# Differential attention by pairs of heads with tokens on the partitions, and a merge that projects its gates ahead of its values

## The reference, cut to what matters

```python
def diffattn_prep(q, k, v, q_norm_w, k_norm_w, rope):
    qh = rmsnorm(q.reshape(bsz, n, B_HEADS, 2, B_QK), q_norm_w)      # B_QK = 64: two maps per head
    kh = rmsnorm(k.reshape(bsz, n, B_HEADS, 2, B_QK), k_norm_w)
    if rope is not None:                                             # latent tokens alone
        qh, kh = apply_axial_rope(qh, rope), apply_axial_rope(kh, rope)
def attend(q, k, v, lam):
    s = einsum('bhmqd,bhmkd->bhmqk', q, k) * (B_QK ** -0.5)
    p = softmax(s, axis=-1)
    w = p[:, :, 0] - lam * p[:, :, 1]
    return einsum('bhqk,bhkv->bhqv', w, v)                           # 128 values per head
def diffattn_out(o, subln_w, lam_init):
    return rmsnorm(o, subln_w) * (1.0 - lam_init)
y_b = diffattn_out(o_b, subln_w, lam_init) * silu(bz)
y = sigmoid(g_a) * (y_a @ w_a_out) + sigmoid(g_b) * (y_b @ w_b_out) + sigmoid(g_c) * (y_c @ w_c_out)
```

## Time and profile before

| | us |
|---|---|
| median of three runs | 2843.8 |
| the profiled execution's own time | 2846.33 |
| its span | 2844.5 |
| branch B and its merge, layer 0, from the first q to the first projection of branch C | 465.7 to 947.6 |
| the same, layer 1 | 1509.5 to 1814.7 |

### The profile page before, as it was taken

How to read it: one execution, slowest core, us unless ns; L and a number is a source line. 1 busy time by engine, 2 the same in 40 slices (tenths; PEclk the granted TensorE clock), 3 DMA queues, 4 the chain that set the end, 5 groups by cost and what they waited for, 6 DMA issues and landing times.

```text
span 2844.5 us, 38559 instructions
## 1 busy us (share of the span) xinstructions
PE 2526.8 (89%) x16000; PEld 2196.4 (77%) x16000; DVE 1299.1 (46%) x2636; ACT 1061.0 (37%) x1815; POOL 850.0 (30%) x554
## 2 busy tenths in 40 slices
PE   6999899988869999968989987997888999888998
PEld 3877778766647888758878776997867899857998
DVE  4322222555542111453234665226665675565673
ACT  3233322433431232333334444443344444354443
POOL 2222222221112233223233222443312354312453
PEclk9899899999979999979989998998999999989999
DMA  6211134111103312222223211444313354402444
GB/s 235 78 60 60 45 119 158 65 45 45 45 30 124 143 60 89 82 78 90 75 91 132 75 66 54 149 143 156 129 49 119 119 179 171 147 36 91 162 171 141
DMA packets 50414, 291.79 MB, mean 103 GB/s; under 512 B 8960, under 2 KB 13184, under 8 KB 19072
## 3 DMA queue, kind: packets, MB, share of 16 engines
q1 hardware_dynamic: 50240, 289.33, 28.6%
HBM read 287.21 MB, written 2.36 MB: 102 GB/s over the span
## 4 chain that ended last, share of the span: by engine, by line
PE 73%; DVE 13%; ACT 7%; issue 2%; POOL 2%; DMA 2%; SPq 1%; DVEq 0%; ACTq 0%; POOLq 0%
PE PS L430 72%; ACT wh L1207 3%; ACT TM L1197 2%; DVE TM L1693 2%; DMA raw<-in_wpk 2%; DVE wl L1712 1%; PE PS L434 1%; POOL wl L2392 1%; DVE TM L1701 1%; POOL TM L2384 1%; DVE small L1697 1%; DVE colS L1701 1%; DVE colS L1974 1%; ACT wh L1208 1%; DVE HYl L1701 1%
## 5 line engine op out<-in xcount | busy, mean ns | idle before, releaser
L430 PE MATMUL PS<-HYh,wh 128*128 128x256 f32 (+1 forms) x3512 | 1155.9, 329 | 65.2 <-DVE HYl L1701 23.1
L430 PE MATMUL PS<-HYl,wh 128*128 128x256 f32 (+1 forms) x3512 | 1132.9, 323 | 0.0
L430 PE MATMUL PS<-HYh,wl 128*128 128x256 f32 (+1 forms) x3512 | 1132.0, 322 | 0.0
L2392 POOL TENSOR_TENSOR wl<-raw,wh 128x768 fp32r<-128x768 f32 (+2 forms) x254 | 578.1, 2276 | 1502.2 <-ACT wh L1208 1502.1
L430 PEld LDWEIGHTS PS<-HYh,wh 128*128 128x128 f32 x3512 | 684.0, 195 | 147.8 <-issue 34.2
L1712 DVE TENSOR_TENSOR wl<-raw,wh 128x1280 fp32r<-128x1280 f32 (+2 forms) x254 | 368.9, 1452 | 767.4 <-ACT wh L1207 767.4
L430 PEld LDWEIGHTS PS<-HYh,wl 128*128 128x128 f32 x3512 | 683.0, 194 | 46.5
L430 PEld LDWEIGHTS PS<-HYl,wh 128*128 128x128 f32 x3512 | 684.5, 195 | 43.1
L1207 ACT ACTIVATE wh<-raw 128x1280 fp32r<-128x1280 f32 (+2 forms) x254 | 306.1, 1205 | 371.6 <-PE PS L430 208.4
L1197 ACT ACTIVATE TM<-PS 128x512 f32<-128x512 f32 (+4 forms) x323 | 164.6, 520 | 738.5 <-PE PS L430 614.5
L430 PE MATMUL PS<-TM 128*128 128x256 f32 (+4 forms) x688 | 220.8, 528 | 95.9 <-DVE TM L1701 53.8
(11 more groups left out here) (155 smaller groups left out, 2205.2 us busy)
## 6 DMA issues: line engine op xcount, KB each, us to landing
raw<-in_wpk SPq DMA_DIRECT2D x235, 1024.0 KB, 4.8
raw<-in_wpk SPq DMA_DIRECT2D x32, 704.0 KB, 4.1
TM<-in_wpk SPq DMA_DIRECT2D x4, 1024.0 KB, 18.7
X<-in_xin SPq DMA_DIRECT2D x1, 2048.0 KB, 10.3
Y<-in_wpk SPq DMA_DIRECT2D x2, 1024.0 KB, 23.7
Y<-bias_d SPq DMA_DIRECT2D x4, 512.0 KB, 10.0
raw<-in_wpk SPq DMA_DIRECT2D x3, 512.0 KB, 3.8
T<-in_tabs SPq DMA_DIRECT2D x1, 1216.0 KB, 15.3
```

The costliest lines, as they stand in the source:

```text
L430: return P.x.matmul(o, l, r, start=start, stop=stop)
L2392: G.x.tensor_tensor(wl[:, s, c:n], raw[:, r, c:n], wh[:, s, c:n], ALU.subtract).then_inc(*lo_rest.mark(u))
```

## The change

Branch B now goes by pairs of heads (p = 0 to 3), with units `b_q`, `b_k`, `b_v`, `b_z` of 256 features each, all projected by `proj_k` in chunks of 128 tokens: 16 chunks per pair in layer 0, 12 in layer 1 (q and z of the latent tokens alone). The norms are then sums along the free axis on VectorE (no `sums`, no `spread`), the rotary embedding is products on GpSimd with tables laid out per token (the features of a head are reordered in the weights so that its halves are contiguous), q and k are transposed by TensorE, v isn't. The values have the weights' transposes as the stationary operand, so that the output has queries on the partitions; its norm is a per-partition scale, and the result is transposed for the merge. Silu and Sigmoid are made from Tanh (the factor of one quarter is in `b_scale`).

The slot tables say which tile is issued in which slot: in layer 0 a tile's scores every second slot, its transposes two slots later, its values three; in layer 1 every third slot, with the same two and three. For the last pair (from its second tile) they lie in the merge, a tile per slot in layer 0 and every second slot in layer 1. The merge `merge_b` projects its eight gates first, a slot before each, and then the values; the first two values leave out the last head's part until it is there.

The table of constants is no longer 768 columns from memory: the small columns are set by memset, and the first load brings 128 columns. A new buffer `wtab` of 512 columns holds the rotary tables per token.

```diff
+        for p in range(4):
+            for tag, base in (("b_q", 4112), ("b_k", 5136)):
+                add(tag, [("w_in", l, [base + 256 * p + 64 * i + d for i in range(4) for d in halves])])
+            for tag, base in (("b_v", 6160), ("b_z", 7184)):
+                add(tag, [("w_in", l, r(base + 256 * p, base + 256 * p + 256))])
+        for j in range(4):
+            add("m_b", [("w_in", l, r(11280 + 256 * j, 11536 + 256 * j))])
...
+        for j in range(4):
+            add("m_b", [("w_b_out", l, r(256 * j, 256 * j + 256))])
...
+        B_PER, B_LAG, B_NT = (16, 12), (14, 11), (4, 2)
...
+            kinds = [("q", t) for t in range(i0, 4)] + [(x, t) for x in "kv" for t in range(4)] + [("z", t) for t in range(i0, 4)]
...
+        def b_score_slot(l, p, j):
+            n = B_PER[l] * p + B_LAG[l] + (2, 3)[l] * j
+            if p == 3 and j:
+                n = 63 + j if l == 0 else 47 + 2 * j
+            return n
+        def b_turn_slot(l, p, j):
+            return b_score_slot(l, p, j) + (1 if l == 0 and p == 3 and j else 2)
+        def b_value_slot(l, p, j):
+            return b_turn_slot(l, p, j) + 1
...
+        B_QK = ({12: 0, 14: 1}, {10: 0, 11: 1})
```

TensorE, a pair's slots and chunks:

```diff
+                for n in range(B_BASE[l]):
+                    p, kind, t_ = b_chunk(l, n)
+                    i, half = divmod(t_, 2)
+                    slot_b(l, n)
+                    if (a := B_QK[l].get(n % B_PER[l])) is not None:
+                        for c, x in enumerate("qk"):
+                            P.wait_ge(pool_step, ("b_ready", l, p, x, 1))
...
+                                t = turned(bank(6 + c)[:, 128 * tt:128 * tt + 128], b_qn[c][:, tt, 128 * a:128 * a + 128])
...
+                    u = place["b_" + kind, 4 * l + p]
+                    proj_k(bank(b)[:, 256 * half:256 * half + 256], u, H, h_ready(l), 8, 128 * t_, ("b_" + kind, l, p, t_),
+                           *([("unit", u)] if t_ == 3 else []))
```

VectorE, `slot_b(l, n, chunk)` with `chunk` = n - 1, in this order on the engine (after `b_exp` come the reciprocal, the product with lambda, the tensor_scalar and the scalar_tensor_tensor as before, which give `b_w`):

```diff
+                if pj := B_SCORES[l].get(n):
+                    D.x.reduce_max(st[:, 32:34], PS[:, 2:4, 0:nk], AX).then_inc(*dve_step.mark())
+                    D.wait_own(dve_step)
+                    ts(st[:, 34:36], st[:, 32:34], -0.125, None, ALU.mult, None, ("b_nb", l, *pj))
+                if chunk is not None:
+                    chunk_b(l, chunk)
+                if pj := B_TURNS[l].get(n + 1):
+                    D.wait_ge(act_step, ("b_exp", l, *pj))
...
+                if (pj := B_VALUES[l].get(n)) and pj[1] % B_NT[l] == B_NT[l] - 1:
+                    D.wait_ge(act_step, ("b_osq", l, *pj))
+                    root(small[:, 40:40 + nt], small[:, 44:44 + nt], colC[:, 32:32 + nt])
...
+                    for i in range(nt):
+                        stt(b_yt[:, i], bank(5)[:, 128 * i:128 * i + 128], small[:, 40 + i:41 + i], b_z[p % 2][:, 2 * l + i, a], ALU.mult, ALU.mult,
+                            ("b_yo", l, p, a))
+            def chunk_b(l, n):
+                if t_ % 2:
+                    if kind in "qk":
+                        D.wait_ge(act_step, ("b_sq", l, p, kind, i))
+                        D.x.reduce_sum(ss[:, 8 * i:8 * i + 8], qn[i], AX).then_inc(*dve_step.mark())
+                        if i:
+                            root(colS[:, z0:16], colS[:, 16 + z0:32], ss[:, z0:16])
+                            for x in range(z0 // 8, 2):
+                                tt(qn[x], wide(bank(b_bank(l, kind, x))), colS[:, 8 * x:8 * x + 8].unsqueeze(2).to_broadcast([128, 8, 64]),
+                                   ALU.mult, ("b_norm", l, p, kind, x))
+                    elif kind == "z":
+                        stt(zt, zt, 1.0, src, ALU.add, ALU.mult, ("b_z", l, p, i))
+                if t_ == 3:
+                    used("b_" + kind, 4 * l + p)
```

GpSimd, after the last chunk of a q or a k: one product of 512 columns (context half), four of 128 (the exchanged halves), two of 256, one sum of 512 (`b_ready`), and then the conversion of its share of a unit:

```diff
+                            tt(x, x, ones(b_w[:, c], 8), ALU.mult)
...
+                                tt(m2[:, :, s_], x[:, :, 1 - s_], b_tab[:, c, 1, t, 32 * s_:32 * s_ + 32].unsqueeze(1).to_broadcast([128, 4, 32]), ALU.mult)
...
+                            tt(x, x, ones(b_tab[:, c, 0, t], 4), ALU.mult)
...
+                        tt(b_qn[c][:, 2:4], b_qn[c][:, 2:4], b_m2, ALU.add, ("b_ready", l, p, kind, 1))
+                    if t_ == 3:
+                        used("b_" + kind, 4 * l + p)
```

ScalarE squares q and k (Square, 512 columns), copies v, makes z's Tanh, each followed at a kind's last chunk by its conversion (`used`); then in the slot it copies the transposed output, the transposed weights, makes the exponentials, and squares a tile's output with its sum (`b_osq`), in this order. The merge on TensorE:

```diff
+                for j in range(8):
+                    u = place["m_b", 8 * l + j // 2]
+                    slot_b(l, base + j)
...
+                    proj_t(bank(j % 2)[:, 0:N], u, 128 * (j % 2), 128, H, h_ready(l), 0, 8, t0, N, ("m_gate", l, "b", j),
...
+                for j in range(2):
+                    slot_b(l, base + 8 + j)
+                    value(u, j, range(7))
+                slot_b(l, base + 10)
+                for j in range(2):
+                    value(u, j, range(7, 8))
...
+                for j in range(2, 8):
+                    value(u, j, range(8))
...
-            S.x.dma_start(T[:, 0:768], tabs[:, 0:768]).then_inc(*consts_in.mark("first", by=16))
+            S.x.dma_start(ident, tabs[:, 0:128]).then_inc(*consts_in.mark("first", by=16))
```

More of the change, by code:

```diff
@@ L52, in merge @@
                 ada(q)
+    halves = [32 * g + 16 * s + k for s in range(2) for g in range(2) for k in range(16)]
     for l in range(2):
@@ L67, in plan_units @@
         merge("a", 10256)
[L68 to L73, removed]
+        for p in range(4):
[5 more added lines that the diff above has]
+            add("m_b", [("w_in", l, r(11280 + 256 * j, 11536 + 256 * j))])
+            if l == 0:
+                ada(ada_at(l, "b", j))
+        for j in range(4):
+            add("m_b", [("w_b_out", l, r(256 * j, 256 * j + 256))])
+            if l == 0:
+                ada(ada_at(l, "b", 4 + j))
         for g in range(4):
@@ L251, in tab @@
             return T[:, at[0] - n:at[0]]
-        ident, o1024, o64, o128, o256, one = (tab(128) for _ in range(6))
+        ident, o1024, o64, o128, o256, one = (tab(n) for n in (128, 1, 2, 1, 4, 4))
         CS = tab(1536).rearrange("p (t c) -> p t c", t=2)
@@ L387, in b_kept @@
[L387 to L391, removed]
+        b_qn = [tm(1024 * c, [4, 256]) for c in range(2)]
+        b_m2 = tm(2048, [2, 256])
+        b_qt = [tm(2560 + 1024 * a, [2, 512]) for a in range(2)]
+        b_v = [tm(4608 + 1024 * i, [4, 2, 128]) for i in range(2)]
+        b_z = [tm(6656 + 1024 * i, [4, 2, 128]) for i in range(2)]
+        b_wt = [tm(8704 + 512 * i, [512]) for i in range(2)]
@@ L1184, in tensor_program @@
                 branch_b(l)
[L1185 removed]
+                merge_b(l)
                 branch_c(l)
@@ new lines, in branch_b @@
+            def branch_b(l):
+                li = 0.8 - 0.6 * math.exp(-0.3 * l)
+                ts(small[:, 34 + l:35 + l], vcol(f"sub{l}"), 0.25 * (1.0 - li), None, ALU.mult, None, ("b_scale", l))
+                D.wait_ge(pe_step, ("b_tables", l))
+                if l == 0:
+                    cp(b_cs.rearrange("p s t d -> p (s t d)"), bank(6)[:, 0:256])
+                else:
+                    D.wait_ge(pool_step, ("b_ready", 0, 3, "k", 1))
+                cp(perm1, bank(6)[:, 256:384], ("b_tables", l))
+                for n in range(B_BASE[l]):
+                    slot_b(l, n, n - 1 if n else None)
@@ L2349, in second_block @@
                 low(name, 7)
+            D.x.memset(o64, 0.0).then_inc(*dve_step.mark())
+            D.wait_own(dve_step)
+            for i in range(2):
+                D.x.memset(o64[64 * i:64 * i + 64, i:i + 1], 1 / 64).then_inc(*dve_step.mark("halves"))
             D.wait_ge(consts_in, "first")
@@ L2582, in pool_program @@
                 branch_b(l)
-                merge(l, "b")
+                merge_b(l)
                 branch_c(l)
```

632 lines of the change are left out of this document (336 added, 296 removed).

## The result

The changed kernel takes 2796.7 us (median of 4 runs, 2790.7 to 2797.7) against 2843.6 (4 runs, 2841.7 to 2844.8): a ratio of 0.9831, 95% interval 0.9814 to 0.9848. It is faster by 47 us, 1.7%, where I forecast 115, and it lies outside my range of 2672 to 2770. The profiled execution took 2796.6 us, its span is 2794.8.

What follows compares the result with a forecast made beforehand. TensorE, busy 89% of the span, was taken as the bound, with its waits and the slow clock after them. Savings of 101 us (layer 0), 13 (layer 1) and 0.5 (table load) gave 115: median 2729 us, range 2672 to 2770.

Steps and rivals of the forecast that it cites:

- Part 2: Branch B's merges: the drain goes, as tiles fit between gates; 6 us of waits left in each merge.
- stretch like 812 to 857: Layer 0's drain before the change: 45.5 us, 19.5 busy, clock 0.64; slots 34 to 40 without projection; forecast to vanish.
- rival (e): Drain stays because the merge's order fails; layer 1 keeps 10 and layer 0 26 us of idling; 2775 us, chance 0.07.
- Part 1: TensorE's work in branch B at full pace: layer 0 from 396 to 362 us, layer 1 from 263 to 235.
- Part 3: Layer 0's pairs: waits behind VectorE's q and k work, 3.3 us per pair, 10 in three; layer 0 takes 381.
- Part 4: Layer 1's pairs: VectorE's queue causes waits of 8, 3.4 and 1.8 us per pair; layer 1 takes 292 us.
- the one I named: Layer 1's pairs: TensorE waits 7 to 8 us before a weights' transpose for VectorE's scalar_tensor_tensor, three times.
- rival (a): Layer 1's waits don't bite because VectorE's chain is shorter than summed; 2680 us, chance 0.17.
- rival (c): Tanh is not in Exp's table set, so slots reload tables, some 25 us; 2754 us, chance 0.05.
- Part 5: GpSimd's rotary products take 5.8 us per q or k, upper bound some 12; ScalarE is not near.
- rival (d): GpSimd becomes the bound through its q and k products, slower than before; about 2860 us, chance 0.03.
- Rival (b): VectorE is later than summed through more waits for GpSimd, 50 us, half on TensorE's path; 2755 us, chance 0.13.

Runs made afterwards that it cites:

- e3: Changed kernel with ScalarE's and VectorE's conversions of the merge's next unit moved behind the following slot; 2746.1 us, ratio 0.9652.
- e2: Changed kernel with VectorE's joining of the two maps ahead of its work on z, q and k in a slot; 2766.0 us, ratio 0.972.
- e8: Changed kernel with the drain put back: all the last pair's slots issued before the merge's first gate; 2788.5 us, ratio 0.9806.
- e9: Changed kernel with only VectorE's conversion in the merge moved behind its slot, ScalarE's left in place; 2783.6 us, ratio 0.9785.
- e1: Changed kernel with layer 0's merge doing the `ada` units before gates 0, 2, 4, 6 instead of after 1, 3, 5, 7; 2757.2 us, ratio 0.9696.
- e6: Changed kernel with the edits of e3 and e2 together, but the merge's first slot in the old order; 2710.4 us, ratio 0.9533.
- e7: As e6, with VectorE's conversion of `b_q` and `b_k` one slot later, behind the next joining; 2707.0 us, ratio 0.9519.

## Why the prediction was wrong

**The step that failed is Part 2's "I leave 6 us of waits in each merge".** The drain did go, and no stretch like 812 to 857 is left, but TensorE waits 29.4 us in layer 0's merge and 14.6 in layer 1's (2.5 of them just before its gate 0), and runs slow behind them. I had listed for each tile its chain of scores, maximum, exponentials and joining (5.7 us of 8.1), and I had put one conversion of VectorE into the account. I did not put in ScalarE's conversion, nor ask when the load that it waits for lands. In the kernel before, these conversions waited for their loads too. Between 812 and 947.6 us there are seven such waits; six of them, of 7.5 to 7.8 us, stand between gates and values, with no slot behind them. The first lies in the drain, and TensorE waits behind it (ScalarE's conversion, and TensorE's next instruction):

```profile
820.29 1.27 ACT L1207 ACTIVATE wh<-raw 128x1280 fp32r<-128x1280 f32 x1 [8.05 <-DMA raw<-in_wpk]
```

```profile
823.10 1.87 PE L430 MATMUL PS<-T,TM 128*128 128x1 f32 x8 [10.32 <-ACT TM L1197]
```

So some 8 of the 26 us of idle time that I put down to slots without a projection between them were a late load already, and the trace of before had shown the cost that I left out. Moving work behind a waiting instruction made its wait critical. My own rival (e), 2775, with chance 0.07, is nearest in kind, and I had no mechanism for it: its price of 26 us of idling for layer 0 was about right (29.4), for layer 1 it was 10 (14.6), and the clock came on top. The sign that I had named for it, a wait in the merge above 4 us, was there five times (5.48, 5.02, 10.12, 4.04, and 5.49 in layer 1).

**Right:** Part 1, TensorE's work: with the waits gone (e3) layer 0 takes 381.1 us, by 362 at full pace and 19 of losses. To the microsecond is luck: TensorE is busy 365.8 us of them and idle 15.3. Part 3: waits of 11.2 us in layer 0's pairs where I had 10. Part 4's queue: 8.02, 3.76 and 1.70 us where I had 8, 3.4 and 1.8; the pairs take 233.9, where 231 were left for them (292 less the merge of 61). A pair of heads took 63.6 and 64.9 us, where I had 63; the work in that sum should have been 12 x 2.90 + 2 x 6.2 = 47.2, not 46.4. The longest wait of branch B outside the merges is the one I named, three times (the longest of all, 10.12 us, is in layer 0's merge), and e2 shows that VectorE's order is its cause, which also ends rival (a). Tanh: branch B and its merge in layer 0 show one table load where the kernel before had 21, so rival (c) falls. The Trainium skill (ScalarE: Activation LUTs, Table sets) lists the two in one set; the trace agrees with it.

```profile
L1284 ACT ACT_TABLE_LOAD x1 | 1.3, 1283 | 0.0
```

**Part 5 was too low, at no cost.** GpSimd's products for a k of layer 0 began at 538.79 and ended at 546.49, 7.7 us, above the 7 that I gave as the limit: GpSimd's groups, 510 to 726 us.

```profile
L2525 POOL TENSOR_TENSOR TM<-TM,wtab 128x128 f32<-128x128 f32 x24 | 19.1, 824 | 0.9
L2525 POOL TENSOR_TENSOR TM<-TM,wtab 128x256 f32<-128x256 f32 x12 | 8.6, 738 | 0.5
L2525 POOL TENSOR_TENSOR TM<-TM 128x512 f32<-128x512 f32 x6 | 7.7, 1290 | 0.5
```

The contiguous ones are what the columns say (0.738 and 1.290); the four with swapped halves take 0.824 in the mean, in place of the 0.45 I gave them. The swapped halves are not the reason. Of the four of one k the shortest takes 0.45 and the first 1.51, and that one begins while VectorE's subtraction runs (durations in ns, least, median and most; and VectorE):

```profile
L2525 POOL TENSOR_TENSOR TM<-TM,wtab x6: 452/733/1513, 540.2 to 544.4; 128x128 f32<-128x128 f32 x4, 128x256 f32<-128x256 f32 x2
```

```profile
539.23 2.20 DVE L1823 TENSOR_TENSOR wl<-raw,wh 128x1280 fp32r<-128x1280 f32 x1
```

The same holds for all six q and k from 510 to 726 us: 1.51 to 1.52 for the first of the four, 0.45 for the second. VectorE's subtraction takes 1.48 to 1.49 in layer 1's merge, with no product beside it. TensorE never waited for GpSimd's q or k in layer 0's pairs, and rival (d) falls with that.

**Rival (b) was half right.** VectorE does wait for GpSimd, and each of the four tiles of layer 1's merge loses 1.4 us so; in the pairs I had allowed 0.6 twice, and their sums held within 0.4 us per wait. The Trainium skill (GPSIMD Engine Reference, Key points) says that the two share SBUF interfaces, with contention when VectorE's instruction has two SBUF inputs or a 2-port mode. The one-column product has two, and the trace agrees: 1.62 us for 0.16.

**Not settled: the last 8 us.** The rest has the same instructions and nearly the same idle time (110.9 us in the changed kernel, 109.6 before), but TensorE is busy 927.1 us for the same 6814 matmuls in place of 920.2. It is the granted clock (0.93 and 0.94 in the rows above). In the other kernels this stretch takes 1029.4 (e8), 1033.1 (e9), 1034.9 (e1) and up to 1039.3 us (e6), in one profile of each. As e8 has the same code there as the changed kernel and takes 1029.4, the code of this stretch is not the cause; what decides when the clock falls was not tried, and I had put the rest at nothing.

## What to carry to other kernels

When work is moved behind another instruction of the same queue, ask of every instruction that it now follows what that one waits for, loads above all: a conversion that waits 7 us for its load is free at the end of a stage and costs the whole wait, and the slow clock after it, in front of a softmax. Put conversions behind the latency-bound chain of their slot and the chain ahead of bulk work on VectorE; these edits (e7) brought 2796.7 - 2707.0 = 90 us here, about twice the change itself. A load queue in order of use with two buffers makes every load wait for whoever holds the buffer of the load ahead of it.

## What the runs showed of the hardware

Some small VectorE instructions that begin while GpSimd's conversion runs end with it: the one-column product takes 1.58 to 1.62 us in four tiles of layer 1's merge, and a 128x2 tensor_scalar, with one input from SBUF, does so as well, ending at 1732.68 where GpSimd ends at 1732.66 (timelines of VectorE and of GpSimd, the changed kernel):

```profile
1730.87 1.81 DVE L1808 TENSOR_SCALAR small<-colC 128x2 f32<-128x2 f32 x1
```

```profile
1730.24 2.42 POOL L2533 TENSOR_TENSOR wl<-raw,wh 128x768 fp32r<-128x768 f32 x1 [7.30 <-ACT wh L1295]
```

A reciprocal beside such a conversion takes 0.15 us (1684.68, in the rows of the result), and a reduction from PSUM in e3 that begins at 1652.65, while GpSimd's runs from 1651.05 to 1653.44, takes 1.23, as the 1.21 to 1.23 elsewhere. So some VectorE instructions wait and some don't, and it isn't a matter of two SBUF inputs alone. It works the other way too: GpSimd's product of 1.51 us above is beside VectorE's subtraction, which itself takes 2.20 there in place of 1.49.

Short idle times don't convert one to one. In e9 and e3 layer 1's merge differs by 2.0 us of idle time and by 6.2 us of time, at clocks of 0.90 and 0.97; in e7 3.5 us less idling of layer 1's pairs gave 0.6 us.
